# One plain block instead of two ahead of the half-size products of a fused encoder block

## The reference

```
x = x + concat(rmsnorm(lru branch), rmsnorm(window attention)) @ w_out
h = rmsnorm(x, g_ffn)
x = x + square(relu(h @ w_ff1)) @ w_ff2          # w_ff1: 1024 x 4096, w_ff2: 4096 x 1024
x = x + sigmoid(rmsnorm(x, g_ple) @ w_ple_gate) * (p @ w_ple_proj)
return rmsnorm(x, g_final)
```

## Time and profile before

| | us |
|---|---|
| median of 3 runs | 1031.58 (1031.29 to 1032.45) |
| profiled execution | 1030.97 |
| span of its trace | 1029.2 |
| PE busy | 1021.0 |
| DVE, ACT, POOL busy | 765.8, 526.0, 500.0 |
| first plain block on PE | 289.15 to 311.80 |
| second plain block | 311.80 to 333.58 |
| first block of seven products | 333.58 to 352.62 |

### The profile page before, as it was taken

The page is one execution under the profiler, slowest core; times in us unless marked ns, Lnnn a source line. Parts: engine busy times, 40 slices in busy tenths (PEclk is TensorE's granted clock), DMA queues, the critical chain, the costliest instruction groups (busy, mean ns, idle before and its releaser), DMA issues.

```text
span 1029.2 us, 13894 instructions
## 1 busy us (share of the span) xinstructions
PE 1021.0 (99%) x4780; PEld 836.2 (81%) x4780; DVE 765.8 (74%) x906; ACT 526.0 (51%) x940; POOL 500.0 (49%) x350
## 2 busy tenths in 40 slices
PE   9999999999999999999999999999999999999997
PEld 7877788777888888888888888888888888888897
DVE  7988787888798787787787777865875765754658
ACT  7567745655677534334434355443555463653234
POOL 0000052343304797887887556444656555741221
PEclk9999999999999999999999999999999999999998
DMA  9111102102003667767767698568985564600004
GB/s 347 43 31 53 41 0 93 41 9 72 3 1 133 243 238 263 277 241 266 278 242 259 242 349 320 202 207 285 321 266 167 192 199 151 218 1 1 1 1 164
DMA packets 63980, 166.28 MB, mean 162 GB/s; under 512 B 6960, under 2 KB 9008, under 8 KB 61872
## 3 DMA queue, kind: packets, MB, share of 16 engines
q1 hardware_dynamic: 63088, 164.43, 45.7%
q10 hardware_dynamic: 832, 1.05, 0.3%
HBM read 115.12 MB, written 50.33 MB: 161 GB/s over the span
## 4 chain that ended last, share of the span: by engine, by line
PE 99%; DMA 0%; DVE 0%; ACT 0%; issue 0%; SPq 0%; DVEq 0%
PE bank L815 32%; PE bank L817 31%; PE bank L816 31%; PE bank L930 1%; PE bank L960 1%; PE bank L901 1%; PE bank L945 1%; PE bank L885 0%; DMA vec<-in_vectors 0%; PE bank L881 0%; DVE xT L2334 0%; PE bank L914 0%; PE bank L882 0%; PE bank L1154 0%; PE bank L1151 0%; PE bank L846 0%
## 5 line engine op out<-in xcount | busy, mean ns | idle before, releaser
L815 PE MATMUL bank<-h_hi,w_hi 128*128 128x512 f32 (+1 forms) x574 | 220.9, 385 | 0.1
L816 PE MATMUL bank<-h_lo,w_hi 128*128 128x512 f32 (+1 forms) x574 | 217.0, 378 | 0.0
L817 PE MATMUL bank<-h_hi,w_lo 128*128 128x512 f32 (+1 forms) x574 | 216.9, 378 | 0.0
L773 POOL TENSOR_TENSOR left_lo<-left_raw,left_hi 128x512 fp32r<-128x512 f32 x88 | 124.9, 1427 | 105.1 <-ACT left_hi L1532 104.8
L2161 DVE TENSOR_TENSOR right_lo<-right_raw,right_hi 128x512 fp32r<-128x512 f32 x88 | 119.0, 1366 | 56.5 <-ACT right_hi L1533 56.2
L815 PE MATMUL bank<-right_hi,left_hi 128*128 128x512 f32 x352 | 136.9, 389 | 0.0
L816 PE MATMUL bank<-right_lo,left_hi 128*128 128x512 f32 x352 | 136.9, 389 | 0.0
L817 PE MATMUL bank<-right_hi,left_lo 128*128 128x512 f32 x352 | 136.9, 389 | 0.0
L815 PEld LDWEIGHTS bank<-h_hi,w_hi 128*128 128x128 f32 x574 | 108.0, 188 | 28.4 <-issue 6.3
L817 PEld LDWEIGHTS bank<-h_hi,w_lo 128*128 128x128 f32 x574 | 108.0, 188 | 20.3
L816 PEld LDWEIGHTS bank<-h_lo,w_hi 128*128 128x128 f32 x574 | 108.0, 188 | 19.7 <-issue 0.5
(11 more groups left out here) (250 smaller groups left out, 2032.9 us busy)
## 6 DMA issues: line engine op xcount, KB each, us to landing
w_raw<-in_w_ff SPq DMA_DIRECT2D x28, 512.0 KB, 5.4
right_raw<-u_b SPq DMA_DIRECT2D x56, 256.0 KB, 4.4
w_set<-in_w_ff SPq DMA_DIRECT2D x26, 512.0 KB, 5.6
w_sums<-w_set SPq DMA_DIRECT2D x13, 1024.0 KB, 3.9
left_raw<-w_sums SPq DMA_DIRECT2D x48, 256.0 KB, 3.9
left_raw<-in_w_ff SPq DMA_DIRECT2D x40, 256.0 KB, 3.0
u_b<-u SPq DMA_DIRECT2D x16, 512.0 KB, 3.0
u_t<-usq SPq DMA_DIRECT2D x16, 512.0 KB, 6.4
```

What stands on the lines that cost most here:

```text
L773: pool.tensor_tensor(left_lo[o][:, :], left_raw[o][:, :], left_hi[o][:, :], ALU.subtract).then_inc(left_ready, 1)
L815: pe.matmul(o, whi, hh, start=first, stop=False, skip_group_check=onto)
L816: pe.matmul(o, whi, hl, start=False, stop=False, skip_group_check=onto)
L817: return pe.matmul(o, wlo, hh, start=False, stop=last, skip_group_check=onto)
```

## The change

`PLAIN` goes from 2 to 1, so 15 blocks instead of 14 are done by seven products, and the second plain block's 96 matmuls become 84. What fed that block (its weight split, its four relus, its part of the squares) goes. The token sums are made straight from `xT` by one instruction each, so ACT scales only four tiles into `x_scale` instead of sixteen. They are all made ahead of the first relus. Products 0 to 6 of block 1 follow the one plain block directly. POOL starts the first block's weights once `t_made[2]` stands at 4. The order of ACT and DVE around it is new.

```diff
-PLAIN = 2
+PLAIN = 1
-FIRST_FF = ((1, 2, 0, 3), (4, 5, 1, 2))
+FIRST_FF = ((1, 2, 4, 5),)
@@ POOL
-            pool.wait_ge(w_split, 2 * FF_FIRST + 3)
-            low(2 * FF_FIRST + 3)
+            pool.wait_ge(t_made[2], LT)
+            w1_prepare((1, 0, 1), 1, 32)
             w1_prepare((2, 0, 1), 0, 32)
@@ PE
+            pe.wait_ge(t_ready[1], LT)
+            pe.wait_ge(t_ready[2], LT)
             for i in range(PRODUCTS):
-                if i < 4:
-                    pe.wait_ge(u_scaled, (3, 7, 4, 8)[i])
-                if i < 4:
-                    pe.wait_ge(t_ready[(2, 2, 1, 3)[i]], LT)
-                if i == 6:
-                    pe.wait_ge(t_ready[4], LT)
-                product(2, i)
+                if i in (1, 3):
+                    pe.wait_ge(u_scaled, 2 if i == 1 else 1)
+                if i in (3, 6):
+                    pe.wait_ge(t_ready[(3, 4)[i // 6]], LT)
+                product(PLAIN, i)
@@ ACT
-            piece_free(act, 10)
-            high(2 * FF_FIRST + 2)
-            high(2 * FF_FIRST + 3)
             root(SS_FFN + 1, 7, r_ffn, D)
-            for k in range(KD):
-                ffn_scale(k, 1)
...
+            first, second = (PLAIN, 0, 1), (PLAIN + 1, 0, 1)
+            t_high_part(1, (0, 1))
+            act.wait_ge(main_done, A0 + 16)
+            act.wait_ge(w_split, 2 * (FF_FIRST + 1))
+            w1_high_part(first, 1, 32, 0)
+            t_high_part(1, (2, 3))
+            t_high_part(2, (0, 1))
+            square_b22((0, 0, 1))
+            w1_high_part(first, 1, 32, 1)
+            w1_high_part(first, 1, 32, 2)
+            t_high_part(2, (2, 3))
+            square_b12((0, 0, 1))
+            w1_high_part(first, 1, 32, 3)
+            w1_high_part(first, 1, 32, 4)
+            t_high_part(3)
+            first_bank(first)
+            t_high_part(4)
+            for hf in range(2):
+                act.wait_ge(u_scaled, 4)
+                act.activation(bank[4 + hf][:, :], r_ffn[:, half(hf)], ACT.Copy).then_inc(r_banked, 1)
             square_b11((0, 0, 1))
...
             act.wait_ge(t_ready[3], LT)
             for i in range(5, PRODUCTS):
-                w1_high_part((2, 0, 1), 0, 32, i)
+                w1_high_part(first, 1, 32, i)
+            square_b21((0, 0, 1))
+            ff_block(first, 0, 32, False)
@@ DVE
+            for i in (3, 1):
+                for k in range(LT):
+                    t_make(i, k)
+            for k in range(LT):
+                t_make(2, k)
+                t_low(1, k)
             first_relu(0, 1)
...
+            for k in range(LT):
+                t_make(4, k)
+                if k == 1:
+                    first_relu(0, 0)
+                t_low(2, k)
             sum_t3((0, 0, 1))
             for k in range(LT):
-                t_make(1, k)
+                t_low(3, k)
+            invert(SS_FFN + 1, r_ffn)
             first_relu(0, 2)
             first_relu(0, 3)
```

More of the change, by code:

```diff
@@ L576, in load_step @@
                 sp.dma_start(right_raw[o][:, :], src).then_inc(ring_in[RING_SEM[o]], 16)
+            sp.wait_ge(main_done, A0 + 16)
+            load_w1(w1_pairs[0, 1], 1)
             spill_b22((0, 0, 1), u_b22[0, 0])
@@ L1389, in ffn_scale @@
                 act.wait_ge(main_free, A0 + 8 * hf + k + 1)
-                if hf == 1 and k >= LT:
-                    act.wait_ge(h_ready, H_PLE)
-                act.activation(raw_h(k, hf), xT[:, k, half(hf)], ACT.Copy, scale=v_ffn[:, k:k + 1]
+                act.activation(x_scale[:, k, :], xT[:, k, half(hf)], ACT.Copy, scale=v_ffn[:, k:k + 1]
                                ).then_inc(ffn_scaled, 1)
@@ L1533, in step_high @@
                 act.activation(right_hi[o][:, :], right_raw[o][:, :], ACT.Copy).then_inc(right_high, 1)
-            square_b11((0, 0, 1))
-            t_high_part(1, (0, 1))
-            act.wait_ge(ff1_done, 4)
-            act.wait_ge(w_split, 2 * (FF_FIRST + 2))
-            w1_high_part((2, 0, 1), 0, 32, 0)
-            square_b21((0, 0, 1))
-            t_high_part(1, (2, 3))
-            t_high_part(2)
-            for i in range(1, 5):
-                w1_high_part((2, 0, 1), 0, 32, i)
@@ L1545, in _ @@
-            first_part(1)
-            t_high_part(3)
-            for hf in range(2):
-                act.activation(bank[4 + hf][:, :], r_ffn[:, half(hf)], ACT.Copy).then_inc(r_banked, 1)
-            t_high_part(4)
+            first, second = (PLAIN, 0, 1), (PLAIN + 1, 0, 1)
[5 more added lines that the diff above has]
+            t_high_part(2, (0, 1))
@@ L1550, in _ @@
+            square_b11((0, 0, 1))
             act.wait_ge(t_ready[3], LT)
             for i in range(5, PRODUCTS):
-                w1_high_part((2, 0, 1), 0, 32, i)
-            first_bank((2, 0, 1))
-            square_b11((1, 0, 1))
-            square_b21((1, 0, 1))
-            ff_block((2, 0, 1), 1, 32, False)
-            ff_block((3, 0, 1), 0, 64)
-            with act.Fori(1, 6) as g:
-                ff_block((2, g, 2), 1, 32 * g + 32)
+                w1_high_part(first, 1, 32, i)
@@ L1560, in _ @@
+            square_b21((0, 0, 1))
+            ff_block(first, 0, 32, False)
+            with act.Fori(0, 6) as g:
+                ff_block((2, g, 2), 1, 32 * g + 64)
                 ff_block((3, g, 2), 0, 32 * g + 64)
-            ff_block((14, 0, 1), 1, 32 * 7)
+            ff_block((14, 0, 1), 1, 32 * 8)
             first_bank((15, 0, 1))
@@ L2093, in w2_sum, with hidden @@
                 dve.tensor_tensor(out, one, other, op).then_inc(made, 1)
-            def hidden(b, sums=True, last=False):
+            def hidden(b, sums=True, last=False, over=None, summed=None):
                 u2, c22, c12, c11, c21 = late[:, 1, :], u22[:, 0, :], usq[:, 0, :], late[:, 0, :], relu[:, 0, :]
                 def product_over(i):
-                    dve.wait_ge(prod_done, at_block(b, PRODUCTS, i + 1 - 2 * PRODUCTS))
+                    dve.wait_ge(prod_done, at_block(b, PRODUCTS, i + 1 - PLAIN * PRODUCTS))
                 def set_sums(pair):
@@ L2120, in hidden @@
                     set_sums(1)
-                else:
-                    sum_t1((1, 0, 1))
-                    sum_t2((1, 0, 1))
-                    sum_t4((1, 0, 1))
+                if over is not None:
+                    over()
                 product_over(3)
-                dve.wait_ge(p5_read, at_block(b, 1, -1))
+                dve.wait_ge(p5_read, at_block(b, 1, 1 - PLAIN))
                 dve.tensor_tensor(c22, bank[2][:, :], c22, ALU.add).then_inc(c22_made, 1)
-                dve.wait_ge(c22_made, at_block(b, 1, -1))
+                dve.wait_ge(c22_made, at_block(b, 1, 1 - PLAIN))
                 relu_scale(c22, 0, u_scaled)
+                if summed is not None:
+                    summed()
                 product_over(4)
@@ L2189, in ple_low, with fourth_low, first_sums @@
                 split_low(H_PLE + KD * hf + i, xT[:, k, half(hf)], v_ple[:, k:k + 1], k, hf)
+            for i in (3, 1):
[4 more added lines that the diff above has]
+                t_low(1, k)
             first_relu(0, 1)
-            first_relu(0, 0)
-            w_low(2 * FF_FIRST + 2)
-            invert(SS_FFN + 1, r_ffn)
             for k in range(LT):
-                t_make(3, k)
+                t_make(4, k)
+                if k == 1:
+                    first_relu(0, 0)
+                t_low(2, k)
             sum_t3((0, 0, 1))
             for k in range(LT):
-                t_make(1, k)
+                t_low(3, k)
+            invert(SS_FFN + 1, r_ffn)
             first_relu(0, 2)
             first_relu(0, 3)
-            for i in (2, 4):
+            def fourth_low():
                 for k in range(LT):
-                    t_make(i, k)
-            sum_t1((0, 0, 1))
-            sum_t2((0, 0, 1))
-            for k in range(LT):
-                t_low(1, k)
-            sum_t4((0, 0, 1))
-            for k in range(LT):
-                t_low(2, k)
-            first_relu(1, 1)
-            first_relu(1, 0)
-            sum_t3((1, 0, 1))
-            for k in range(2):
-                t_low(3, k)
-            first_relu(1, 2)
-            first_relu(1, 3)
-            for k in range(2, LT):
-                t_low(3, k)
-            for k in range(LT):
-                t_low(4, k)
-            dve.wait_ge(r_banked, 2)
+                    t_low(4, k)
+                dve.wait_ge(r_banked, 2)
+            def first_sums():
+                sum_t1((0, 0, 1))
+                sum_t2((0, 0, 1))
+                sum_t4((0, 0, 1))
+            hidden((PLAIN, 0, 1), False, over=fourth_low, summed=first_sums)
             hidden((2, 0, 1), False)
```

139 lines of the change are left out of this document (63 added, 76 removed).

## The result

| | before | after |
|---|---|---|
| median, us | 1031.84 (6 runs, 1031.2 to 1032.45) | 1049.07 (6 runs, 1048.38 to 1049.98) |
| span of the profiled execution, us | 1029.2 | 1047.2 |

The ratio is 1.0167, 95% interval 1.0154 to 1.018: slower by 17.2 us. Forecast were 1047.0 us and a range of 1041 to 1050.5.

The account below looks back on a forecast made before the run. PE was taken to bound the kernel, with no idle time. Terms -2.72 + 11.4 + 1.0 + 6.0 = +15.7 us on 1030.97 gave 1046.7; with the median 0.6 higher, 1047.0 was predicted, range 1041 to 1050.5.

Parts of the forecast that it names:

- The bound: Whole kernel: PE is busy 1021.0 of 1029.2 us, with no idle time in which a delay could be made up.
- What is saved: Second plain block: 96 matmuls become 84, saving 12 x 0.2267 = 2.72 us; by the records 4.7 us.
- When the second token sum is written: DVE ahead of block 1: t2's fourth tile is written at 310.5 us.
- POOL's first sums: POOL, first block's weights: begin at 310.5, take 5.5 + 2.0 us contention = 7.5, so s2 at 318.0.
- The first stall: PE ahead of block 1: product 0 starts at 323.2 instead of 311.8, 11.4 us.
- The estimate of 5.45 for the four without contention: POOL's s1, a21, low part of slot 0 and s2: 5.45 us together, read from the second block before the change.
- Inside block 1: Product 5, due at 336.8, waits for POOL's low part at 337.8: 1.0 us; block 1 ends at 343.2.
- The second stall: PE ahead of block 2: product 0 waits for c11 at 349.2 after block 1 ends at 343.2, 6.0 us.
- The rival that POOL catches up: Only the first stall: POOL catches up within block 1, the 6.0 us ahead of block 2 go, 1041; chance 0.13.
- The clock: Rival: PE's clock halves after the pauses, hidden behind the first, open behind the second at 2.7 us per product, 1050; chance 0.20.
- The main case: Both stalls and the wait inside block 1, no clock loss: 1047.0 us, own range 1043 to 1048.5; chance 0.60.
- a first stall of 8.5 us: Low end of the stall ahead of block 1, with s2 at 316.0; everything behind moves too, sum +12.8 us.

Follow-up runs that it names:

- e1: Changed kernel with all four tiles of the second token sum ahead of the high parts of slots 1 and 2 in ACT's order: 1048.21 us.
- e2: Changed kernel without POOL's wait for the second token sum: 1049.34 us.
- e6: Changed kernel with 40 extra matmuls on PE in the first gap, result never read: 1048.55 us.
- e3: Changed kernel with ACT's high parts of slots 5 and 6 ahead of its bank 0 copy, and block 2's slot 0 ahead of b21's square: 1042.15 us.
- e4: Changed kernel with 22 extra matmuls on PE in the second gap, result never read: 1046.55 us.
- e12: e5 with b11's square and block 1's first sums earlier, plus ACT's further block 1 squares ahead of block 2's slots 2 to 4: 1039.39 us.
- e11: e5 with b11's square and block 1's first sums earlier, plus t4 made behind t2's low parts and ACT's t4 high parts later: 1044.42 us.
- e5: Changed kernel with the edits of e1 and e3 together: 1043.31 us.
- e8: e5 with 28 extra matmuls on PE in the first gap, result never read: 1042.12 us.

## Why the prediction was right

**The bound.** That PE is the bound and has no idle time to give back was right: the 17.6 us lost by block 3 stand in the span (18.0).

**What is saved.** -2.72, right; read by start-to-start times. The records would have said 4.7.

**When the second token sum is written.** Predicted 310.5, measured 311.1. Of the difference, DVE came to the sums 0.6 us later (301.23), as late as this execution runs from its first stretches on, before anything of the change.

**POOL's first sums.** Predicted 7.5 us from there to s2, measured 5.9 (311.14 to 317.00). The 2.0 us for contention were too much: the four instructions took 1.29, 1.60, 1.71 and 1.26 us, 0.7 above their undisturbed 1.3 each. DVE paid instead: the records of its t4 tiles are 0.81, 1.15, 1.78 and 1.75 us long, where such a record alone is 0.75. The prediction had POOL pay a full tile each time. By the Trainium skill (SBUF — State Buffer, Who interferes with whom) it is whoever issues second that waits, and the rows agree: POOL's s2 began at 315.74 and took 1.26 us, and DVE's tile, 0.03 us behind it, took 1.78.

**The first stall.** Predicted 11.4, measured 10.1, for that reason; the chain from s2 to product 0 was predicted at 5.2 us (318.0 to 323.2) and took 5.5 (317.0 to 322.5). The estimate of 5.45 for the four without contention was close to what they took with it (5.9). e1 confirms ACT's order as a link of it; e2 shows that taking POOL's wait away does not shorten it.

**Inside block 1.** Predicted 1.0, measured 0. The wait was there to be had: e6 shows 1.65 us of it (1.49 by the list) once the clock is held up, and the slow clock, 2.0 us, covered it in after. Block 1 ended at 343.6 (343.33 and one matmul), forecast 343.2: a start 0.7 us earlier than forecast and the wait that did not come make up for the 2.0 us of low clock, which is luck.

**The second stall.** Predicted 6.0, measured 5.4, by the named chain: POOL's seventh low part ended at 339.1 (339.0), s2 at 344.35 (344.6), c11 at 348.95 (349.2), product 0 at 349.0. e3 removes all but 1.15 us of it with two moves in ACT's list. The rival that POOL catches up (1041) is refuted in after; e3 (1042.15) is what it looks like.

**The clock.** This is the step that failed. The main case left the clock out, at a chance of 0.20 for the rival, with the reason that a slow block 1 would shorten the second pause to 3 us or less. It did not: block 1 took up its 2.0 us in the wait that it would have had anyway, the second pause stayed 5.45 us, and the low clock behind it lay open at 2.2 us (the same in e4). The rival's price of 2.7 for a product at the low clock was a little high: at starts 0.427 us apart it is 12 x (0.427 - 0.2267) = 2.4, and the clock came back within one. From the forecast sum one comes to the measured one by the first stall (-1.3), the second (-0.6), the wait inside block 1 (-1.0), the two low clocks (+2.0 and +2.2) and the later start (+0.6): 15.7 - 1.3 - 0.6 - 1.0 + 2.0 + 2.2 + 0.6 = 17.6. That the total was only 2 us off is in part luck: 2.9 us too much in the waits against 4.2 us of clock left out.

Two small slips in the sums change nothing: 1046.7 and 0.6 are 1047.3, not 1047.0, and a first stall of 8.5 us gives 1044.1 as the low end of the main case, not 1043.

The Trainium skill, TensorE: Matmul & The Clock Gate, section Why this matters for your kernels, was the rule that made this the case to expect, and both gaps of after (10.06 and 5.45 us) agree with it.

**What stays open.** Whether any order makes one plain block as fast as two. e12 is 7.5 us short of before, and its first gap ends with DVE's list, which in e1 runs from 300.5 to 319.1 and in which POOL's work costs DVE some 2 us (e1's tiles of t4 at 0.81, 1.16, 1.78 and 1.16 us). Moving parts of that list (e11) gave the gap back later; moving the fourth token sum to POOL or ACT was not tried. Nor is it settled how much of e11's loss is DVE's work and how much the order on ACT, why the spill of `usq` takes 2.7 us in some executions and over 4 in others, and what both orders of e5 give with the faster one and no filling.

## What to carry to other kernels

A block that costs a few matmuls more may be the cover behind which other engines prepare; before it goes, add up what the busiest of them must do in that time, and look at the first gap and the next one, since a wait taken away at one tends to come back at the other (e1, e8, e11). An order on a helper engine that mixes work for now with work for later is where a gap is closed for nothing: two moves in ACT's list were worth 6.9 us (e3), another rearrangement 3.4 (e12). And a gap on PE costs more than its length: count the low clock behind it, by what waits after it. Before a difference between two profiles is put down to the edit, the transfers on the path should be compared too: the same spill took 2.7 us in e3 and 4.4 in e5.
